# A two-block transformer kernel: conditioning vectors as row sums on VectorE, the first norm's squares summed on TensorE, the first input taken by halves of the tokens

## The reference

```python
# first block
mod = silu(c) @ w_ada + b_ada                    # [1, 6 * 1024]
sh1, sc1, g1, sh2, sc2, g2 = split(mod, 6)
h = rms_norm(x, norm_mix_g) * (1 + sc1) + sh1
proj = h @ w_in                                  # 23 tiles of 128 outputs
y = concat(attention(proj), bidirectional_mlstm(proj)) @ w_out
x = x + g1 * y
h = rms_norm(x, norm_ffn_g) * (1 + sc2) + sh2
x = x + g2 * (silu(h @ w_gate) * (h @ w_up)) @ w_down
x = rms_norm(x, final_norm_g)
# second block: mod2 = silu(c_2) @ w_ada_2 + b_ada_2, [1, 3 * 1024], used in the
# same way around two more kinds of attention and an output product
```

## Time and profile before

| What | Value |
|---|---|
| Time, median of 3 runs | 2559.81 us (2553.73 to 2560.52) |
| The profiled execution's own time | 2554.61 us |
| Its span | 2552.8 us |
| Mean granted TensorE clock | 0.951 |
| TensorE (PE) busy | 2269.8 us (89%) |
| TensorE weight load (PEld) busy | 1757.0 us (69%) |
| VectorE (DVE) busy | 1207.1 us (47%) |
| ScalarE (ACT) busy | 1002.7 us (39%) |
| GpSimd (POOL) busy | 32.3 us (1%) |
| DMA | 213 MB, mean 83 GB/s |

### The profile page before, as it was taken

The page is one execution under the profiler, slowest core; times in us unless marked ns, Lnnn a source line. Parts: engine busy times, 40 slices in busy tenths (PEclk is TensorE's granted clock), DMA queues, the critical chain, the costliest instruction groups (busy, mean ns, idle before and its releaser), DMA issues.

```text
span 2552.8 us, 25453 instructions
## 1 busy us (share of the span) xinstructions
PE 2269.8 (89%) x9776; PEld 1757.0 (69%) x9776; DVE 1207.1 (47%) x1662; ACT 1002.7 (39%) x1442; POOL 32.3 (1%) x79
## 2 busy tenths in 40 slices
PE   6998989988887796888999799999799999999795
PEld 6776866654666674667788678888577777776474
DVE  3584545454666534555433443333443344444544
ACT  2232235455677425222222432222432465444432
POOL 0000000000111000000000000000000000000000
PEclk9999999988889897999999999999899999999897
DMA  5314210101000122433333223233223110102042
GB/s 215 140 58 142 106 58 1 42 0 75 1 1 1 58 70 104 181 148 149 118 119 119 99 91 99 92 127 120 82 91 117 49 42 17 42 9 107 0 150 98
DMA packets 57383, 213.04 MB, mean 83 GB/s; under 512 B 5936, under 2 KB 7088, under 8 KB 52400
## 3 DMA queue, kind: packets, MB, share of 16 engines
q1 hardware_dynamic: 57264, 211.41, 24.1%
HBM read 183.60 MB, written 25.17 MB: 82 GB/s over the span
## 4 chain that ended last, share of the span: by engine, by line
PE 66%; DVE 15%; ACT 10%; issue 5%; DMA 4%; SPq 1%; POOL 0%; DVEq 0%; ACTq 0%; POOLq 0%
PE ps L852 14%; PE ps L854 14%; PE ps L853 14%; PE ps L1005 7%; DMA w_raw<-in_weights 3%; PE ps L1068 2%; ACT w_hi L1184 2%; PE ps L861 2%; PE ps L981 2%; DVE w_lo L1581 2%; PE ps L982 2%; PE ps L949 2%; DVE acc_a L1600 2%; DVE y L1654 2%; ACT x1c L1451 1%
## 5 line engine op out<-in xcount | busy, mean ns | idle before, releaser
L852 PE MATMUL ps<-h_hi,w_hi 128*128 128x512 f32 x1504 | 621.2, 413 | 106.3 <-DVE w_lo L1581 81.6
L854 PE MATMUL ps<-h_hi,w_lo 128*128 128x512 f32 x1504 | 600.7, 399 | 0.0
L853 PE MATMUL ps<-h_lo,w_hi 128*128 128x512 f32 x1504 | 600.2, 399 | 0.0
L1581 DVE TENSOR_TENSOR w_lo<-w_raw,w_hi 128x1024 fp32r<-128x1024 f32 x216 | 264.4, 1225 | 443.7 <-ACT w_hi L1184 443.6
L852 PEld LDWEIGHTS ps<-h_hi,w_hi 128*128 128x128 f32 x1504 | 291.7, 194 | 193.9 <-DVE w_lo L1581 99.8
L1184 ACT ACTIVATE w_hi<-w_raw 128x1024 fp32r<-128x1024 f32 x216 | 227.3, 1053 | 392.9 <-DMA w_raw<-in_weights 205.1
L854 PEld LDWEIGHTS ps<-h_hi,w_lo 128*128 128x128 f32 x1504 | 290.6, 193 | 64.6
L853 PEld LDWEIGHTS ps<-h_lo,w_hi 128*128 128x128 f32 x1504 | 292.1, 194 | 59.1 <-issue 2.4
L1725 DVE TENSOR_REDUCE mh<-ps 128x1 f32<-128x512 f32 x192 | 125.0, 656 | 174.2 <-PE ps L949 96.9
L1005 PE MATMUL ps<-full_pf,full_v 128*128 128x512 f32 x256 | 135.9, 613 | 4.0 <-ACT full_pf L1322 4.0
L852 PE MATMUL ps<-hid_hi,w_hi 128*128 128x512 f32 x352 | 136.9, 389 | 0.0
(11 more groups left out here) (276 smaller groups left out, 3281.8 us busy)
## 6 DMA issues: line engine op xcount, KB each, us to landing
w_raw<-in_weights SPq DMA_DIRECT2D x216, 512.0 KB, 3.6
wa<-in_ada SPq DMA_DIRECT2D x36, 1024.0 KB, 4.8
m_scratch<-y SPq DMA_DIRECT2D x12, 512.0 KB, 2.9
xt<-in_x SPq DMA_DIRECT2D x2, 2048.0 KB, 10.8
y<-m_scratch SPq DMA_DIRECT2D x4, 1024.0 KB, 5.9
x_again<-in_x SPq DMA_DIRECT2D x8, 512.0 KB, 3.6
x_scratch<-x SPq DMA_DIRECT2D x2, 2048.0 KB, 10.1
x1c<-x_scratch SPq DMA_DIRECT2D x16, 256.0 KB, 3.8
```

The source lines that it names most:

```text
L852: e.matmul(o, w_hi[slot][:, tile_of(kw)], hi, start=start, stop=False)
L853: e.matmul(o, w_hi[slot][:, tile_of(kw)], lo, start=False, stop=False)
L854: return e.matmul(o, w_lo[slot][:, tile_of(kw)], hi, start=False, stop=stop)
L1581: return e.tensor_tensor(dst, src, hi.bitcast(F32), ALU.subtract)
```

## The change

Outputs go on partitions: the conditioning matrix is stored with one row of 1,024 inputs for each output, and silu(c) is loaded as a row on every partition (`cond`). One VectorE instruction then multiplies a tile of 128 rows by it and sums along the row, with the bias as the start value (`ada`); there are 72 such rows, with loads of 512 KB each. The first 16 are loaded two at a time into eight buffers right behind x, the others into three buffers in turn; the load of row o waits for the sum of row o−3. TensorE has no part in the conditioning. The squares of x are summed by 16 matmuls with ones in two banks (`x_squares`), x is not multiplied in place, and h is made half of the tokens by half, in 16 slices of 512. TensorE takes the first two projection tiles in the order tile 0 first half, tile 1 first half, tile 0 second half, tile 1 second half. x is loaded first.

On SyncE's queue each load of a row stands right behind the portion in which VectorE sums the row that it waits for.

```diff
+def portions(kind, out, tiles, place, paired=False):
 
 
     fill, due = [], []
-    for t in tiles:
-        for n in range(2):
-            for part in range(3):
-                steps, due = due, []
-                if n == 0 and part == 0:
-                    steps.append(("w", place(t) + 1))
-                steps.append((kind, t, n, part))
-                if part == 2:
-                    due = [(out, t, n)]
-                fill.append(steps)
+    halves = [(t, n) for t in tiles for n in range(2)]
+    if paired:
+        halves[1:3] = halves[2:0:-1]
+    for t, n in halves:
+        for part in range(3):
+            steps, due = due, []
+            if part == 0 and n == (1 if paired and t == tiles[1] else 0):
+                steps.append(("w", place(t) + 1))
+            steps.append((kind, t, n, part))
+            if part == 2:
+                due = [(out, t, n)]
+            fill.append(steps)
...
-    fill = portions("proj", "y1", IN1_ORDER, IN1_ORDER.index)
+    fill = portions("proj", "y1", IN1_ORDER, IN1_ORDER.index, True)
...
-    for n, i in enumerate((1, 7, 13, 21, 27, 33, 39, 68, 73, 78, 83, 88)):
-        put(0, max(0, i - 5), ("adal", 8 + n))
-        put(0, i, ("adav", 8 + n))
-        put(0, i + 4, ("ada", 8 + n))
+    places = (12, 13, 14, 15, 19, 22, 25, 28, 31, 34, 37, 40, 46, 52, 58, 66, 68, 70, 72, 74, 76, 78, 80, 82, 84, 86, 88, 95, 101, 107,
+              110, 112)
+    for n, i in enumerate(places):
+        put(0, places[n - 3] + 1 if n >= 3 else 0, ("adal", 16 + n))
+        put(0, i, ("ada", 16 + n))
...
+    p.add("ada_rows")
+    for step in (("xsq", 0), ("xsq", 1), ("xr", 0), ("xr", 1)):
         p.add(*step)
+    for o in range(16):
+        p.add("ada", o)
+    p.add("mod1")
+    p.add("h", 0)
+    p.add("h", 1)
...
-    extras = norm_steps("ffn", 1) + [("adal", 20), ("adal", 21)]
-    for i in range(20, 36):
-        extras += [("adav", i)] + ([("adal", i + 2)] if i + 2 < 36 else []) + [("pause",), ("ada", i)]
+    extras = norm_steps("ffn", 1) + 7 * [("pause",)] + [("cond",)] + [("adal", o) for o in range(48, 51)]
+    for o in range(48, 72):
+        extras += [("ada", o), ("adal", o + 3) if o + 3 < 72 else ("pause",)]
...
-        cmask = Area(0, 64)("cmask", [P, 5, P], F32)
+        cmask = Area(161, 164)("cmask", [P, 5, P], F32)
         xt = Area(64, 96)("xt", [P, KT, T], F32)
-        ada_area, early = Area(156, 174), Area(130, 156)
-        wa = [ada_area(f"wa{i}", [P, KT, CW], F32) for i in range(2)]
-        wa += [early(f"wa{i}", [P, KT, CW], F32) for i in range(2, 5)]
-        area, again = Area(120, 136), Area(152, 168)
-        wa += [area(f"wa{i}", [P, KT, CW], F32) for i in range(5, 7)] + [again(f"wa{i}", [P, KT, CW], F32) for i in range(7, 9)]
-        acc_a = [Area(173, 174)("acc_a0", [P, CW], F32)]
+        area = Area(0, 64)
+        ada_first = [area(f"ada_first{i}", [P, 2, D], F32) for i in range(8)]
+        area, again = Area(120, 132), Area(152, 164)
+        ada_next = [area(f"ada_next{i}", [P, D], F32) for i in range(3)] + [again(f"ada_last{i}", [P, D], F32) for i in range(3)]
+        cond = [Area(132, 136)("cond0", [P, D], F32), Area(164, 168)("cond1", [P, D], F32)]
         area = Area(0, 64)
         h_hi = area("h_hi", [P, KT, T], F32R)
         h_lo = area("h_lo", [P, KT, T], F32R)
         area = Area(96, 130)
-        sq = [area(f"sq{i}", [P, HT], F32) for i in range(2)]
-        wide = [area(f"wide{i}", [P, T], F32) for i in range(2)]
-        acc = [area(f"acc{i}", [P, HT], F32) for i in range(2)]
+        sq = [area(f"sq{i}", [P, HT], F32) for i in range(4)]
+        wide = [area(f"wide{i}", [P, HT], F32) for i in range(4)]
+        area = Area(157, 161)
         rstd = [area(f"rstd{i}", [P, HT], F32) for i in range(2)]
...
+        def ada_place(o):
+
+            if o < 16:
+                return ada_first[o // 2][:, o % 2, :], s[f"ada_first{o // 4 if o < 8 else o // 2 - 2}"], 32 if o < 8 else 16
+            return ada_next[(o - 16) % 3 + (3 if o >= 48 else 0)][:, :], s[f"ada_in{(o - 16) % 3}"], 16 * ((o - 16) // 3 + 1)
...
-            def ada(i):
-                bank = ada_bank(i)
-                if i < 20:
-                    aux_free(("ada", i))
-                    e.wait_ge(s["norm_ln"], 2)
-                else:
-                    e.wait_ge(s["ada_mod"], i - 7)
-                e.wait_ge(s["ada_acc"], KT * (i - 7))
-                for h in range(2):
-                    x = e.matmul(ps[:, bank, h:h + 1], ada_sum(i)[:, h * P:(h + 1) * P], ones[:, 0:1], start=True, stop=True,
-                                 skip_group_check=True)
-                x.then_inc(s["ada_mm"], 1)
+            def x_squares(n):
+                e.wait_ge(s["const_in"], 48)
+                for k in range(KT):
+                    e.wait_ge(s["sq_made"], KT * n + k + 1)
+                    e.matmul(ps[:, 4 + n, :], ones[:, :], sq[k % 4][:, :], start=(k == 0), stop=(k == KT - 1)).then_inc(s["acc_made"], 1)
...
                 for k in range(3 * part, min(3 * part + 3, KT)):
-                    if chunk == 1:
-                        e.wait_ge(s["h_lo"], k + 1)
+                    if t == IN1_ORDER[0]:
+                        e.wait_ge(s["h_lo"], KT * n + k + 1)
                     x = three(ps[:, bank, :], i % 2, k, h_hi[:, k, half_of(n)], h_lo[:, k, half_of(n)], k == 0, k == KT - 1)
                 if part == 2:
...
 
             def start():
-                e.wait_ge(s["small_in"], 16)
-                e.activation(cs[:, :], small[:, 0:16], ACT.Silu).then_inc(s["cs_made"], 1)
+                condition(0)
+                exp_tables()
+
+            def condition(n):
+                e.wait_ge(s["cond_in"], 16 * (n + 1))
+                e.activation(cond[n][:, :], cond[n][:, :], ACT.Silu).then_inc(s["cond_made"], 1)
 
             def round_weights(i):
...
+                    if KT * n + k >= 4:
+                        e.wait_ge(s["acc_made"], KT * n + k - 3)
+                    e.activation(sq[k % 4][:, :], xt[:, k, half_of(n)], ACT.Square).then_inc(s["sq_made"], 1)
 
             def inverse_root(r, bank, dst):
 
-                e.wait_ge(s["norm_mm"], r)
+                e.wait_ge(*((s["norm_mm"], r - 2) if r > 2 else (s["acc_made"], KT * r)))
                 e.activation(dst[:, :], ps[:, bank, :], ACT.Ln, bias=col("eps"), scale=1.0 / D).then_inc(s["norm_ln"], 1)
                 e.wait_ge(s["norm_ln"], r)
                 e.activation(dst[:, :], dst[:, :], ACT.Exp, scale=-0.5).then_inc(s["norm_r"], 1)
 
...
                 for k in range(KT):
-                    e.wait_ge(s["h_pre"], k + 1)
-                    copy(h_hi[:, k, :], wide[k % 2][:, :]).then_inc(s["h_hi"], 1)
+                    e.wait_ge(s["h_pre"], KT * n + k + 1)
+                    e.activation(h_hi[:, k, half_of(n)], wide[k % 4][:, :], ACT.Identity, bias=mod1[:, k:k + 1]).then_inc(s["h_hi"], 1)
...
-            def ada_rows(i):
-
-                buffer, landed, value = ada_place(i)
-                acc_t, vec, done = ada_sum(i), 0 if i < 24 else 8, KT * (i - 8)
+            def ada(o):
+
+                rows, landed, value = ada_place(o)
+                m, i, b = (mod1, o, SMALL["b_ada"][0]) if o < 48 else (mod2, o - 48, SMALL["b_ada_2"][0])
                 e.wait_ge(landed, value)
...
-                    tt(xt[:, k, half_of(n)], xt[:, k, half_of(n)], rstd[n][:, :], ALU.mult).then_inc(s["x_scaled"], 1)
+                e.wait_ge(s["cond_made"], 1 + o // 48)
+                if o == 0:
+                    e.wait_ge(s["small_in"], 16)
+                e.tensor_tensor_reduce(rows, rows, cond[o // 48][:, :], 1.0, small[:, b + i:b + i + 1], ALU.mult, ALU.add,
+                                       m[:, i:i + 1]).then_inc(s["ada_done"], 1)
...
             def mod_first():
-                o = SMALL["b_ada"][0]
-                e.wait_ge(s["ada_mm"], 8)
-                tt(mod1[:, 0:16], ps[:, 7, 0:16], small[:, o:o + 16], ALU.add).then_inc(s["ada_mod"], 1)
-                e.wait_ge(s["ada_mod"], 1)
+                e.wait_ge(s["ada_done"], 16)
                 scale_col(s_mix, "norm_mix_g", mod1, 8).then_inc(s["scale_made"], 1)
                 e.memset(xp_two[1][:, 0:2], 0.0).then_inc(s["pad_made"], 1)
                 e.memset(xp_two[1][:, 2 + T:4 + T], 0.0).then_inc(s["pad_made"], 1)
 
-            def h():
+            def h(n):
+                def low(k):
+                    e.wait_ge(s["h_hi"], KT * n + k + 1)
+                    e.scalar_tensor_tensor(h_lo[:, k, half_of(n)], wide[k % 4][:, :], mod1[:, k:k + 1], h_hi[:, k, half_of(n)].bitcast(F32),
+                                           ALU.add, ALU.subtract).then_inc(s["h_lo"], 1)
+
                 e.wait_ge(s["scale_made"], 1)
-                e.wait_ge(s["x_scaled"], 2 * KT)
-                for k in range(KT + 1):
-                    if k < KT:
-                        if k >= 2:
-                            e.wait_ge(s["h_lo"], k - 1)
```

(58 more changed lines are left out.)

108 lines of the change are left out of this document (28 added, 80 removed).

## The result

| What | Before | After |
|---|---|---|
| Time, median of 4 runs each | 2559.7 us | 2588.0 us (2584.6 to 2589.5) |
| Ratio to before, 95% interval | | 1.012 (1.0107 to 1.0133) |
| Span of the profiled execution | 2552.8 us | 2585.8 us |
| Mean granted TensorE clock | 0.951 | 0.937 |
| VectorE (DVE) busy | 1207.1 us | 1172.9 us |

The change costs 28 us. The prediction was 2576, 16 us slower, in a range of 2543 to 2626. The two profiled executions lie 33 us apart, as the one of before is 5 us under its median.

The account below looks back on a forecast made before the run. It took SyncE's waits for sums, queued ahead of weight loads, as what costs time. 27.7 − 29.3 − 7.5 + 5.8 − 12.9 = −16.2, so 16 us slower: 2576 us, range 2543 to 2626.

Parts of the forecast that it names:

- 1. Start: At the start, 16 row sums on VectorE replace the first eight blocks' matmuls: a lead of 27.7 us at tile 4.
- 2. Head tiles: Head normalisation, tiles 4 to 8: SyncE's wait for a row closes a loop of 20.8 us; 29.3 us lost.
- 3. Convolution tiles: Tiles 9 to 11, 17, 18: row and its load lie between convolution and weight load; 7.5 us lost.
- 4. Output-gate tiles: Tiles 12 to 16: three rows a tile, a loop of 9.6 us under TensorE's 10.9; 5.8 us won.
- 5. Gate and up: Gate and up tiles: a row load ahead of each weight load, 21 turns of 8.38 us; 12.9 us lost.
- The bold sentence: Whole kernel: a wait for a sum in SyncE's queue ahead of a weight load is what costs time.
- place (c): First gate and up tiles, old kernel: SyncE's wait for a block's sum closes the loop, 6.89 us a tile against TensorE's 5.44.
- A: Rival: a weight tile behind a 512 KB row lands in 3.6 us, not 4.4; 2548 us, faster; chance 0.20.
- C: Rival: no net change, the start's lead lost in dearer loops; landing at 3.9 gives 2561 us; chance 0.16.
- far case: Far part of the short-landing rival: SyncE's waits bind nowhere, some 80 us won; chance 0.03.
- B: Rival: the row sum on VectorE runs at half rate, 2.3 us; 46 us more, 2622; chance 0.14.

Follow-up runs that it names:

- e1: Changed kernel with each gate and up row load moved one tile later, behind the next weight load: 2524.3 us, ratio 0.9875.
- e2: Changed kernel with row loads in the first projections moved behind the next weight load where the row isn't needed before it: 2536.8 us, ratio 0.9924.
- e7: Changed kernel with the squares of x added on VectorE again, ahead of the 16 rows, one matmul a half: 2598.0 us, ratio 1.0156.
- e4: Changed kernel with the halves of the first two projection tiles in the old order: 2579.5 us, ratio 1.009.
- e5: Changed kernel with the stores of the four output-gate tiles moved to tile 15: 2583.2 us, ratio 1.0103.
- e11: Old kernel with each gate and up block load behind a weight load, waiting for the sum of two tiles ago: 2560.8 us, ratio 1.0012.
- e12: Old kernel with block loads behind weight loads and each block's eight passes in the other tile of each pair: 2524.1 us, ratio 0.9865.
- e6: Changed kernel with later row loads in gate and up and first projections, and the first two tiles' halves in old order: 2465.5 us, ratio 0.9642.

## Why the prediction was right, and where it wasn't

**The cause was right**: row loads that wait for a fresh sum in SyncE's queue, ahead of the next weight load, tie each weight tile to VectorE. e1 and e2 move only those loads and win 63 and 49 us. The size was not: 16 us forecast, 28 measured, and 31 by the low parts. The wide range took that in. Term by term, from the table of low parts:

| Term | Predicted | Measured |
|---|---|---|
| 1. Start, at tile 4 | +27.7 | +27.2 |
| 2. Head tiles, 4 to 8 | −29.3 | −30.3 |
| 3. Convolution tiles, 8 to 12 and 16 to 19 | −7.5 | −10.2 |
| 4. Output-gate tiles, 12 to 16 | +5.8 | −4.4 |
| Between 19 and 36 | 0 | +2.6 |
| 5. Gate and up, from tile 36 | −12.9 | −16.3 |
| Sum, at tile 174 | −16.2 | −31.4 |

1. The terms nearly hold: first row 24.2 for 22.7 (the landing as its bytes give it, without the 1.5 us taken off for x's earlier issue), the 16 rows 19.7 us for 20.8, h 22.1 for 22, TensorE's restart at 67.8 for 67.5, and the squares under the rows (e7). The clock behind the restart took 2.9 us (the 0.18 that was not granted, times the 16.3 us in e4's row) for 1.7. The three terms as written, 28.2 − 1.7 + 3 × 0.34, make 27.5 and not 27.7.

2. A turn is 21.3 for 20.8: TensorE's sum 3.8 for 3.4, the landing 4.35 for 4.4, the row 1.2.

4. **This step failed, by 10 us.** The prediction had two rows ahead of the weight load and yet let it land in 4.4, the price behind one row. ScalarE and SyncE's queue after:

```profile
261.17 1.06 ACT L1157 ACTIVATE w_hi<-w_raw 128x1024 fp32r<-128x1024 f32 x1 [8.48 <-DMA w_raw<-in_weights]
...
273.48 1.06 ACT L1157 ACTIVATE w_hi<-w_raw 128x1024 fp32r<-128x1024 f32 x1 [9.91 <-DMA w_raw<-in_weights]
```
```profile
254.94 11.32 SPq L2020 DMA_DIRECT2D ada_next<-in_ada  x3
266.30 0.43 SPq L2014 DMA_DIRECT2D w_raw<-in_weights  x1
266.83 0.38 SPq L2034 DMA_DIRECT2D m_scratch<-y  x1
```

The tile issued at 266.30 lands at 273.48, 7.2 us. Put that in place of 4.4 and the loop of 9.6 becomes 12.4; measured 12.3 (261.17 to 273.48). It is then above TensorE's 10.9, so four turns take 47.8 us where 37.5 were expected, and the stage that was to win loses. e5 gives the store 1 us of the 7.2; the rest above the lone 3.4 stands with the two rows issued within 1.6 us ahead.

3 and 5. Here the size was off by 3 us each. In gate and up the 21 turns took 178.6 us for 176: most took 8.3, three took 9.3 to 10.0, as their weight tiles landed in 5.3 to 6.1 us and not 4.3, for a reason that no run shows. The first turn began 1.2 later than worked out. Over the convolution tiles, e2's later loads gave back 8.4 of the 10.2 us; a change there alone wasn't tried. The 2.6 us between tiles 19 and 36 stay open.

**One reason was wrong though its number served.** The bold sentence on what costs time was said of the old kernel too, for place (c). e11 removes that wait there and wins nothing; e12 moves VectorE's passes as well and wins 35 us. The trace of before showed it, in ScalarE's timeline:

```profile
1062.92 0.63 ACT L1184 ACTIVATE hid_hi<-gated 128x512 fp32r<-128x512 f32 x1 [6.73 <-DVE gated L1577]
1063.46 1.04 ACT L1184 ACTIVATE w_hi<-w_raw 128x1024 fp32r<-128x1024 f32 x1
```

It waits 6.7 us for VectorE's gated product and rounds the weight tile at once after it, with no wait for the load. That is one tile of each pair. In the other ScalarE does wait for the load, but TensorE doesn't idle for it. TensorE's timeline has one stall a pair, ahead of the tile behind the gated product, and none where the load came late (the pair's other tile starts at 1058.03, straight behind the matmuls before it):

```profile
1052.04 0.50 PE L852 MATMUL ps<-h_hi,w_hi 128*128 128x512 f32 x1 [2.08 <-DVE w_lo L1581]
...
1058.03 0.48 PE L852 MATMUL ps<-h_hi,w_hi 128*128 128x512 f32 x1
...
1065.81 0.50 PE L852 MATMUL ps<-h_hi,w_hi 128*128 128x512 f32 x1 [2.08 <-DVE w_lo L1581]
```

The prediction didn't read these rows and took the wait that it saw for the one that bound. For the forecast this changed nothing, since the pace of 6.89 was taken from rows. But it means that the row sums took away a bound on VectorE (4.0 us of passes a pair of tiles became 1.2 a tile), and that their order put one on SyncE in its place.

**The rivals.** A's short landing didn't come (4.3 to 7.2), nor C's, which needed 3.9. Its far case, in which SyncE's waits bind nowhere, was given 0.03 and some 80 us; it is what e6 makes true by moving steps, with 8 us more from the halves: 91. B falls by the row's 1.21 us from start to start.
